# An encoder layer on one core: the first expert's remaining chunks gathered by twos between its matmuls, and the sum of the first logits moved ahead of a turn

## The reference

```
h = rmsnorm(x); proj = h @ w_in + b_in            # queries, keys, values, gates
x = x + (sigmoid(ga) * (A @ w_branch_a) + sigmoid(gb) * (B @ w_branch_b)) @ w_out
h2 = rmsnorm(x)
logits = h2 @ router_w + router_b                 # 32 experts
top_val, top_idx = top_k(logits, 4); probs = softmax(top_val)
for e in range(32):
    gate = min(h2 @ w_gate[e] + b_gate[e], 7)
    up = clip(h2 @ w_up[e] + b_up[e], -7, 7)
    act = gate * sigmoid(1.702 * gate) * (up + 1)
    y += combine[:, e] * (act @ w_down[e] + b_down[e])
x = rmsnorm(x + y)
```

## Time and profile before

| | |
|---|---|
| Median of 3 runs | 1160.91 us (1160.1 to 1161.3) |
| Profiled execution | 1161.57 us, of which 1159.7 us are span |
| TensorE busy | 1114.7 us, 96% |
| VectorE, ScalarE busy | 368.4 us (32%), 259.8 us (22%) |
| Chain that ended last | PE 72%, DMA 26%, DVE 1% |
| Read from HBM | 443.47 MB, 383 GB/s over the span |

### The profile page before, as it was taken

The page is one execution under the profiler, slowest core; times in us unless marked ns, Lnnn a source line. Parts: engine busy times, 40 slices in busy tenths (PEclk is TensorE's granted clock), DMA queues, the critical chain, the costliest instruction groups (busy, mean ns, idle before and its releaser), DMA issues.

```text
span 1159.7 us, 15058 instructions
## 1 busy us (share of the span) xinstructions
PE 1114.7 (96%) x6117; PEld 553.4 (48%) x6117; DVE 368.4 (32%) x905; ACT 259.8 (22%) x526; POOL 15.6 (1%) x20
## 2 busy tenths in 40 slices
PE   8999999999999999899989898989999999999998
PEld 8998989854343434243424242424343334443333
DVE  5477765642322222121212222121222121222213
ACT  6476556430110111010101111111110111111002
POOL 1000000000000000000000000000000000000000
PEclk9999999999999999999999999998999999999999
DMA  9856557899999999999999999999999999999995
GB/s 287 292 169 188 173 185 284 335 377 409 414 420 428 428 431 429 431 430 430 433 431 431 432 429 429 432 431 431 430 432 432 429 430 431 431 427 430 422 423 229
DMA packets 54221, 445.51 MB, mean 384 GB/s; under 512 B 3875, under 2 KB 32217, under 8 KB 36753
## 3 DMA queue, kind: packets, MB, share of 16 engines
q1 hardware_dynamic: 52106, 439.83, 91.6%
q0 software_dynamic: 1248, 4.20, 1.3%
q10 hardware_dynamic: 806, 0.59, 0.2%
HBM read 443.47 MB, written 1.13 MB: 383 GB/s over the span
## 4 chain that ended last, share of the span: by engine, by line
PE 72%; DMA 26%; DVE 1%; issue 0%; ACT 0%; DVEq 0%; SPq 0%
PE psum L1450 27%; DMA ring<-in_w_up 25%; PE psum L1485 14%; PE psum L1056 5%; PE psum L1369 5%; PE psum L1057 5%; PE psum L1058 5%; PE psum L1384 4%; PE psum L1392 2%; PE psum L1103 1%; PE psum L1196 1%; PE psum L1172 1%; PE psum L1377 1%; PE psum L1150 1%; PE psum L1451 0%; PE psum L1326 0%
## 5 line engine op out<-in xcount | busy, mean ns | idle before, releaser
L1450 PE MATMUL psum<-ring,xT 128*64 128x512 f32 x960 | 435.3, 610 | 36.5 <-DMA ring<-in_w_up 36.5
L1451 PE MATMUL psum<-ring,xT 128*64 128x512 f32 x960 | 435.4, 610 | 0.0
L1450 PEld LDWEIGHTS psum<-ring,xT 128*64 128x64 f32 x960 | 132.2, 141 | 316.1 <-issue 278.9
L1485 PE MATMUL psum<-ring,guT 128*64 128x512 f32 x984 | 224.5, 598 | 0.4 <-DVE guT L1981 0.4
L1962 DVE COPY gu<-psum 128x512 f32<-128x512 f32 x32 | 33.5, 1047 | 573.3 <-PE psum L1451 573.3
L1451 PEld LDWEIGHTS psum<-ring,xT 128*64 128x64 f32 x960 | 132.2, 141 | 0.0
L1485 PEld LDWEIGHTS psum<-ring,guT 128*64 128x64 f32 x984 | 65.3, 136 | 134.0 <-issue 112.0
L995 ACT COPY gu<-psum 128x512 f32<-128x512 f32 x32 | 34.0, 1062 | 423.0 <-PE psum L1451 423.0
L1639 DVE TENSOR_TENSOR low<-raw,high 128x2048 fp32r<-128x2048 f32 x31 | 71.3, 2299 | 35.5 <-ACT high L779 35.4
L1056 PE MATMUL psum<-hT_hi,high 128*128 128x256 f32 x272 | 78.3, 288 | 0.1
L1057 PE MATMUL psum<-hT_lo,high 128*128 128x256 f32 x272 | 76.9, 283 | 0.0
(11 more groups left out here) (219 smaller groups left out, 1029.2 us busy)
## 6 DMA issues: line engine op xcount, KB each, us to landing
ring<-in_w_down SPq DMA_DIRECT2D x25, 4096.0 KB, 21.0
ring<-in_w_up SPq DMA_DIRECT2D x24, 4096.0 KB, 29.2
ring<-in_w_gate SPq DMA_DIRECT2D x23, 4096.0 KB, 30.2
raw<-in_w_in SPq DMA_DIRECT2D x22, 1024.0 KB, 5.3
ring<-in_w_gate SPq DMA_DIRECT2D x11, 2048.0 KB, 23.6
ring<-in_w_up SPq DMA_DIRECT2D x10, 2048.0 KB, 24.2
ring<-in_w_down SPq DMA_DIRECT2D x13, 1024.0 KB, 11.3
ring<-in_w_up SPq DMA_DIRECT2D x12, 1024.0 KB, 10.4
```

The lines of the kernel that those rows point to most:

```text
L1450: mm(every(bank(GU + nb)[0:CAP, :]), x_k, of_chunks(gate[:, k, :], nb), start=k == 0, stop=k == KC - 1)
L1451: done = mm(every(bank(GU + nb)[CAP:P, :]), x_k, of_chunks(up[:, k, :], nb), start=k == 0, stop=k == KC - 1)
L1485: done = mm(o[half * CAP:(half + 1) * CAP, :], values[:, k, :], chunk_k[:, half * BANK:(half + 1) * BANK], start=k == 0, stop=k == KC - 1)
```

## The change

Two parts.

1. `sum_groups(0)` stands ahead of `turn_tokens(1, 0)` and no longer behind it.
2. The second tokens' gather of chunks 2 to 7 is no longer one block behind the expert's matmuls of chunk 0. Chunks 2 and 3 are gathered behind chunk 0, chunks 4 and 5 behind chunk 1, chunks 6 and 7 behind chunk 2. A new semaphore `gather_steps` tells ScalarE of the first two of these steps, and `gather_up` of the third. ScalarE raises a semaphore for each chunk that it has copied, and each of the first expert's chunks on TensorE waits for its own. The gather of chunks 4 and 5 waits until chunk 3 is copied, since it writes the bank that the copies of chunks 2 and 3 read.

```diff
--- before.py
+++ after.py
@@ -89,6 +89,7 @@
 SPLITS = [len(loads) for loads in FIRST] + [len(OPENING) - 1 - sum(c >= KC - EXTRA for c in OPENING[:-1]), len(OPENING) - 1] + [len(THIRD) - 1] + [len(SECOND) - 1] * 2 + [2]
 
 AT_ONCE = 2
+STEPS = KC // AT_ONCE - 2
 EARLY = {2 * RING + 1: 0, 2 * RING + 2: 1, 2 * RING + 4: 2}
 assert HEAD % 2 == 0
 
@@ -412,7 +413,7 @@
             sem(n) for n in ("gu_left", "gu_right", "guT_up", "guT_done", "gate_done", "sig_done", "up_done",
                              "gated_done", "hidden_done", "y_copied"))
         y_up, result_done, y_out = sem("y_up"), sem("result_done"), sem("y_out")
-        y_first, count_read = sem("y_first"), sem("count_read")
+        y_first, count_read, gather_steps = sem("y_first"), sem("count_read"), sem("gather_steps")
         block = ctx.enter_context(nc.Block())
 
         def is_value(p):
@@ -968,20 +969,21 @@
                 for k in range(AT_ONCE):
                     copy_chunk(xT, k, first_gathered(k)).then_inc(xT_first, 1)
 
-            def copy_other_chunks(pair):
-
-                act.wait_ge(gather_up, pair + 1)
+            def copy_other_chunks(pair, p):
+
                 for k in range(AT_ONCE, KC):
-                    last = copy_chunk(xT, k, first_gathered(k))
-                    if k == KC // 2 - 1:
-                        last.then_inc(xT_half, 1)
-                last.then_inc(xT_done, 1)
+                    if k == KC - AT_ONCE:
+                        act.wait_ge(gather_up, pair + 1)
+                    elif k % AT_ONCE == 0:
+                        act.wait_ge(gather_steps, p * STEPS + k // AT_ONCE)
+                    signal = xT_half if k == KC // 2 - 1 else xT_done if k == KC - 1 else xT_first
+                    copy_chunk(xT, k, first_gathered(k)).then_inc(signal, 1)
 
             copy_first_chunks(0)
             act.wait_ge(passes_done, 1)
             n_passes = act.value_load(further[P - 1:P, 0:1], min_val=0, max_val=PASSES - 1) + 1
             with act.Fori(0, n_passes) as p:
-                copy_other_chunks(p * PAIRS)
+                copy_other_chunks(p * PAIRS, p)
                 load_table(2, ACT.Sigmoid)
 
 
@@ -1336,8 +1338,8 @@
             pe.wait_ge(stack_done, 1)
             route(0, 0)
             route(0, 1)
+            sum_groups(0)
             turn_tokens(1, 0)
-            sum_groups(0)
             turn_tokens(1, 1)
             route(1, 0)
             return_tokens(0, 0, 0)
@@ -1421,7 +1423,7 @@
 
 
                 for h in range(PARTS):
-                    if not odd and not (first and h == 0):
+                    if not odd and not first:
                         pe.wait_ge((xT_half, xT_done)[2 * h // PARTS], pair + 1)
                     if m0 >= TAIL:
 
@@ -1442,10 +1444,13 @@
                         k = h * HALF + c
                         if m0 >= TAIL and k == KC - HALF // 2 and nb == 0:
                             pe.wait_ge(tail_in[9 if m0 == TAIL else 7], 32 * (p + 1))
-                        if first and nb == 0 and k < AT_ONCE:
-                            pe.wait_ge(xT_first, p * AT_ONCE + (k + 1))
-                        elif first and nb == 0 and k == AT_ONCE:
-                            pe.wait_ge(xT_half, pair + 1)
+                        if first and nb == 0:
+                            if k == KC // 2 - 1:
+                                pe.wait_ge(xT_half, pair + 1)
+                            elif k == KC - 1:
+                                pe.wait_ge(xT_done, pair + 1)
+                            else:
+                                pe.wait_ge(xT_first, p * (KC - 2) + (k + 1 if k < KC // 2 else k))
                         x_k = tokens[:, k, odd * CAP:(odd + 1) * CAP]
                         mm(every(bank(GU + nb)[0:CAP, :]), x_k, of_chunks(gate[:, k, :], nb), start=k == 0, stop=k == KC - 1)
                         done = mm(every(bank(GU + nb)[CAP:P, :]), x_k, of_chunks(up[:, k, :], nb), start=k == 0,
@@ -1454,11 +1459,12 @@
                             done.then_inc(gu_half, 1)
                         if m0 <= 3 and nb == 1 and k + 1 in (SECOND if m0 else OPENING) and (k + 1) % HALF:
                             done.then_inc(first_used, 1)
-                        if first and k == 0 and nb == 1:
-
-                            gather_first(1, AT_ONCE, AT_ONCE + KC // 2)
-                            pe.wait_ge(xT_first, p * AT_ONCE + AT_ONCE)
-                            gather_first(1, AT_ONCE + KC // 2, KC).then_inc(gather_up, 1)
+                        if first and k <= STEPS and nb == 1:
+
+                            c0 = (k + 1) * AT_ONCE
+                            if c0 == KC // 2:
+                                pe.wait_ge(xT_half, pair + 1)
+                            gather_first(1, c0, c0 + AT_ONCE).then_inc(gather_steps if k < STEPS else gather_up, 1)
                     done.then_inc(used, 2)
                     if gathers is not None and h == PARTS // 2 - 1:
 
```

## The result

Over 22 runs of each kernel the changed one takes 1162.75 us (median; 1161.27 to 1164.85), the one before 1161.32 us (1159.74 to 1163.09). The ratio is 1.0013 with a 95% interval of 1.0007 to 1.0019: **1.4 us slower (0.8 to 2.2), a real loss, but under 0.2%**. The direction was forecast, and "within 0.2%" too; the size was not (+0.5), and the time lies just above the range. Part of that is the base: the three runs that the prediction started from had a median of 1160.91 us, 0.4 under that of the 22.

A forecast was written before the change was run, and what follows sets the result against it. TensorE, then DMA loads bound the kernel, one after the other. TensorE +0.25 + 0.36 = +0.6 us; loads -0.7 + 1.3 = +0.6, taken as +0.5: 1161.57 + 0.5 - 0.66 = 1161.4 us, range 1159.5 to 1162.5.

The forecast's parts named there:

- What bounds where: Whole kernel: up to 461 us TensorE never waits for weights and loads wait for its releases; from there TensorE waits.
- the term that was mis-sized: Gathers in the first expert: three blocks cost 2.04 us against 1.68 for one, so TensorE +0.36 us.
- The doubling that I had allowed for: Upper bound for the gathers by twos: 0.7 us, for waits against register values before chunks 1, 2, 4, 5 and 6.
- The new waits: Waits for ScalarE's copies in the first expert: cost nothing, under the cover of each chunk's four records (1.72 us).
- The releases: First expert's chunk loads: chunk 0 0.25 us later, chunk 1 0.75 earlier, chunk 2 0.1 earlier, chunk 3 and later 0.6 later.
- What the gain was worth: Load stream near 252 us gains 0.7 us (0 to 0.9); asked whether that lasts to 461 us.
- the likeliest case: Loads end late by what TensorE is late, the stream's gain eaten: +0.5 us, chance 0.50.
- the mechanism that I named: Load released at 308.93: 1.3 us less work in front, loss grows up to 1.3 us, nearly one for one.
- the sign that I had named: Load landing around 318 us: the forecast is wrong if it is not later.
- The gap stays filled: Rival 1: the stream's 0.7 us gain lasts until TensorE waits for loads; 1160.2 us, chance 0.24.
- Nothing moves: Rival 2: block borders covered, turn no later, gain at 252 us lost at 308.93; 1160.9 us, chance 0.22.
- Slower: Rival 3: ScalarE's copies don't keep pace, gather blocks wait, sum passes 2.5 us; 1163.5 us, chance 0.03.

The follow-up runs named there:

- The fifth expert's price: Kernel before with the first matmul of each sum in the fifth expert run three times more (5.1 us): 1166.35 us, ratio 1.0033, +3.8 us.
- the full dose: 5.1 us of TensorE work from repeating the first matmul of each sum three times more in one expert; first expert against kernel before: 1166.78 us, ratio 1.0042.
- the cut inside chunk 0: Kernel before with its block of twelve gather records cut into three blocks of four, all inside chunk 0, no new semaphore or wait: 1162.68 us, ratio 1.0012.
- part 2's kernel: Kernel before with only the gathers by twos, order of turn and sum as before: 1162.06 us, ratio 1.0006.
- the dose of the seventh expert: Kernel before with 5.1 us of repeated matmuls in the seventh expert (near 410 us): 1161.83 us, ratio 1.0003.
- a late one: Kernel before with 5.1 us of repeated matmuls in expert 20 (counted from 0): 1161.70 us, ratio 1.0001.

## Why the prediction was right or wrong

*What bounds where.* Right for the first expert, and measured: 5.1 us there cost 4.9, in the seventh 0.3. I had said that lateness counts as long as TensorE waits for no load, up to 461 us. That misreads the row: at 461.20 the load is issued, and TensorE idles for it only from 485.85 to 490.21. And the limit lies earlier than either: the seventh expert, near 410 us, is ahead of TensorE's first long wait, and lateness is nearly free there already. Ten and more us of loads stand in front of an issue by then (the load of 4 MB issued at 421.89 took 19.7 us), so the loads don't fall behind, and TensorE's lateness goes into the wait that ends at 490.21. The fifth expert's price, 2.4 to 5.1 us, can't be told from the full dose.

*Part 1.* +0.25 forecast, bound +0.33, measured +0.34. The mechanism is as told: the turn stands behind a wait that it did not need, VectorE's gain is lost in the wait for the ranking. I took a value near the lower end of 0.23 to 0.33, and the trace has the upper end.

*Part 2, the term that was mis-sized.* +0.36 forecast, +0.69 measured. The step that failed is the price of a block of four: I took 0.53 us from the row 244.43 to 244.96, where a return of tokens follows. Ahead of an expert matmul it is 0.64. The row of the long block could have warned me: 12 records took 1.53 and not 3 x 0.53 = 1.59, so the time of a block is not in proportion to its records. With 1.42 for twelve records (243.07 to 244.49 in the profile after, the same form) against 0.53 for four, a record is (1.42 - 0.53) / 8 = 0.111 us, and 1.53 - 8 x 0.111 = 0.64 is the block of four ahead of an expert matmul. Each added block costs 0.69 / 2 = 0.345 us and not 0.18. The doubling that I had allowed for (0.7) put it down to the waits against register values; the cut inside chunk 0, which has none of them, shows the same 0.53 and 0.64.

*The new waits* cost nothing, as forecast: no wait for `xT` on TensorE, 0.43, 1.88 and 1.88 us of waiting on ScalarE's side.

*The releases.* Chunk 1's load was issued 0.5 us earlier, forecast 0.75, and chunk 2's 0.3 later, forecast 0.1 earlier, both for the same reason: each block in front cost 0.11 more, and part 1 0.1 more. The stream gained 0.75 us there (0.4 to 1.0 against the other executions), forecast 0.7.

*What the gain was worth.* Nothing, as the likeliest case had it, but not by the mechanism that I named. I had put the loss at the load issued at 308.93, nearly one for one with the work in front of it. In part 2's kernel the load ahead of it was issued at 302.70, the next at 309.57:

```profile
ring<-in_w_up SPq DMA_DIRECT2D x1, 2048.0 KB, 9.7
```

```profile
ring<-in_w_down SPq DMA_DIRECT2D x1, 2048.0 KB, 7.8
```

They landed at 312.4 and 317.4, 5.0 us apart, with 2.8 us in front: no loss. In the second execution of the kernel before the two, issued at 302.17 and 309.04, landed at 314.0 and 318.9, 4.9 us apart:

```profile
ring<-in_w_up SPq DMA_DIRECT2D x1, 2048.0 KB, 11.8
```

```profile
ring<-in_w_down SPq DMA_DIRECT2D x1, 2048.0 KB, 9.9
```

The changed kernel's own profile has the two issued at 303.16 (10.1 us to landing) and 310.03:

```profile
ring<-in_w_down SPq DMA_DIRECT2D x1, 2048.0 KB, 9.8
```

They landed at 313.3 and 319.8, about 6.5 us apart, with 3.3 in front. So the sign that I had named, a later landing around 318 us, is there (319.8; five executions without the change have 318.0 to 318.9), but it follows from no rule on the work in front: 2.8 us in front lost nothing, 3.3 lost 1.1 in one profile and 1.6 in another, and the landings of one kernel lie up to 1.8 us apart there. The Trainium skill (page "DMA: Bandwidth & Descriptors", section "Anatomy of one DMA — SWDGE (gpsimd) path") gives about 2 us of fixed cost for a transfer that GpSimd issues. These loads come from the SP queue; 2.8 us in front that lose nothing would agree with it, 3.3 us that lose 1.1 and 1.6 would not.

What the runs do show: the gain is gone by 280 us, ahead of the load that I had named (366 GB/s from 246 us on, against 362 to 372). Over 246 to 461 us the changed kernel's loads move 414 GB/s; four executions of the kernel before, two of them with the dose of the seventh expert (from 408 us on) or of a late one, move 415 to 417. That is 0.5 to 1.5 us of loads less, around TensorE's 1.02. A lateness in the first expert is carried in full (4.9 of 5.1), and later filling at 250 us costs nothing that shows (0.35 us faster with chunk 0's release 1.27 later). Which single load between 258 and 280 us loses the gain stays open.

*The size.* TensorE's lateness, 1.02 us, lies inside the interval of the time's, 0.8 to 2.2. With +0.69 for part 2 and the base of 22 runs the same working (the loads late by what TensorE is late) gives 1161.3 + 1.0 = 1162.3. The rest, 0.4 us, can't be told from nothing, and so it is open whether anything but TensorE's lateness has a part in the loss.

*The rivals.* "The gap stays filled" (1160.2) is out by the result, and by the loads, which at 280 us are no further than before. "Nothing moves" is out by the interval. "Slower", with copies that don't keep pace, is out by the rows of ScalarE.

## What to carry to other kernels

A block of small matmuls put between others has a price for its borders: here about 0.35 us for a block of four records and for one of twelve (1.68 - 12 x 0.111), so cutting one block into three must win more than 0.7 us. Ahead of a step that makes releases earlier, ask what follows if the engine that releases becomes later: TensorE's time in the first expert counted in full, and what was filled of the stream's gap was gone 20 us later. And a known dose (here 5.1 us of repeated matmuls) at a few places tells in which stretch a tenth of a microsecond is worth looking for, when the effect itself is too small for the clock.

## What was not expected of the hardware

Two matmuls of 64 columns of weights each, into the two halves of the partitions, start their records 0.01 us apart and share 0.43 us for each; with other matmuls between them a record that finds no partner takes its own 0.43 (0.86 more for the two pairs that were cut). And the landing of one and the same load differs by up to 1.8 us between two executions of one kernel whose matmuls agree within 0.12 us up to there, so that a single profile's landings don't carry an argument about one microsecond.
